# Gated linear attention: each head's norm follows in pieces during the next head's scan, and the output projection's first tile takes its input tiles as they are finished

## The chip, the core and the metric

The kernel runs on one core of a Trainium2 chip. The metric is the device time of one execution in microseconds (us). The four compute engines of the core work in parallel, each on its own list of instructions in order, and wait for one another through semaphores: TensorE (PE, matrix multiplies; its weight loads are listed apart as PEld), VectorE (DVE), ScalarE (ACT) and GpSimd (POOL). SyncE (SP) issues the DMAs that bring the weights. Everything is float32; the profile has two records for each float32 matmul.

## What is computed

The program is a two-layer backbone over 256 context tokens and 256 latent tokens: layer 0 is a bidirectional chunked gated linear attention (GLA) and a dense SwiGLU, layer 1 a bidirectional RWKV-7 mixer and a top-2-of-8 mixture of experts (MoE). The change is in GLA alone. Cut to what matters:

```
def gla_chunk_scan(q, k, v, log_a, s0):            # chunks of 64 tokens
    def step(s, inp):
        b = cumsum(log_a of the chunk);  q_dec = qc * exp(b)
        att = where(mask, q_dec @ (kc * exp(-b)).T, 0)
        y = att @ vc + q_dec @ s
        s = s * exp(b_last) + (kc * exp(b_last - b)).T @ vc
        return s, y

def finish(y, r):                                  # y: sum of both directions, per head 256 values
    yn = y * rsqrt(mean(y * y, axis=-1) + NORM_EPS) * norm_g
    return (yn.reshape(..., 1024) * silu(r)) @ w_out
```

There are 4 heads of 128 keys and 256 values. What `finish` does for a head needs that head's scan alone; the product with `w_out` sums over all heads.

## The kernel before

Activations lie with features on the 128 partitions and the 512 tokens (context, then latent) along the row, so a tensor of 1024 features is 8 tiles of 128x512. The GLA result is `Y1`, tiles 2h and 2h+1 for head h.

**The scan of a head.** TensorE computes the masked-to-be scores of both directions into PSUM banks `ps[0]` and `ps[1]` (L802, 8 matmuls), VectorE masks and adds them (L1765, L1768, L1771), and TensorE multiplies them with the values into `ps[2]` and `ps[3]` (L810). Then follow 8 steps, i = 0 to 7, with both directions in each. In a step TensorE computes the two state updates of the chunk (L821, into `ps[4]` to `ps[7]`), VectorE makes the new state from the old one and the update (L1781 in step 0, L1784 after that), and from step 1 on TensorE adds the part of the output that the state gives (L831). An update of the state waits until TensorE has read the old one, and L831 of the next step waits for the new one. When step 7 is through, ScalarE copies the two banks to `Y1` (L1378).

**The norm.** It begins when all four heads are scanned and copied. For each head in turn: ScalarE squares the two tiles into `sq` (L1385); TensorE sums the squares over the features with a matrix of ones, two matmuls into `ps[h % 2]` (L840); ScalarE takes the root into the one buffer `std` (L1389); VectorE takes the reciprocal (helper `get_rstd`, L1634) and multiplies twice for each tile: with the reciprocal (L1792), then with the gain and silu(r) (L1793, which counts `fn_done` up). ScalarE's root for a head waits for `fn_done` of the head before it, since `std` is one buffer.

**The projection.** The helper `project` (matmuls at L735) makes 8 output tiles of 8 matmuls each. Before its first one stands a wait for all 8 `fn_done`. From the third tile on it has a sum of squares for the next norm between tiles (helper `stat`, L660). ScalarE empties each tile (helper `empty`, L1333). Weights come through a ring of six slots of 1 MB; SP issues a chunk at L479 when TensorE has finished with the chunk six places before it. The MoE weights have rings of their own, filled from L495 and L502 in the same way.

The order of work is the order in which the code stands, engine by engine; there is no scheduler.

## Time and profile before

| what | value |
|---|---|
| median of 3 runs | 2488.49 us (2486.59 to 2490.86) |
| the profiled execution, its own time | 2480.1 us |
| its span, first to last instruction | 2478.3 us |
| TensorE busy | 2267.4 us, 91% of the span |
| VectorE busy | 657.1 us, 27% |
| ScalarE busy | 454.4 us, 18% |
| mean granted TensorE clock | 0.959 of full |

The profile is one execution. Shares are averages over stages with different limits. From about 1515 us on the MoE weights stream in at up to 407 GB/s; the GLA scan and norm lie between 268 and 375 us, in which hardly a byte is moved. A matmul's busy time is modelled at its end, so neighbouring matmul rows overlap a little; the distance between their starts is the better measure of the pace. Line numbers (L802) are those of the kernel before unless said otherwise.

### The profile page before, as it was taken

Reading aid. Unit: us, or ns where it says so; the run is one execution under the profiler, and the core shown is the slowest. Engines: PE = TensorE matmul, PEld = TensorE weight load, DVE = VectorE, ACT = ScalarE, POOL = GpSimd, SP = SyncE. Lnnn points to the kernel's source line nnn. Section 1 sums busy time; section 2 is a strip of 40 time slices with the busy share of each in tenths; the row PEclk is TensorE's granted clock in tenths of the full one; section 3 lists DMA queues with packets and bytes.
Section 4 is the critical chain, followed back from the end, with each engine's and each line's share of the span. In section 5 each row is a group of like instructions: output and inputs, shape, how many; then the busy total and the mean of one; then the engine's idle time right before and its main releaser. Section 6 shows DMA issues by size and latency. Waiting matters only on the chain.

```text
span 2478.3 us, 43079 instructions
## 1 busy us (share of the span) xinstructions
PE 2267.4 (91%) x19363; PEld 1416.9 (57%) x19364; DVE 657.1 (27%) x1175; ACT 454.4 (18%) x771; POOL 48.5 (2%) x165
## 2 busy tenths in 40 slices
PE   6999879899999999897997997989999989999986
PEld 3474644344446877787877876433776333875332
DVE  1032450400000034776467753210000101000102
ACT  3134111200000116453424433000000000000001
POOL 0000000400000000000000000000000000000000
PEclk8999889999999999999999998999999989999998
DMA  7254101522223362102340025899998999999994
GB/s 260 85 184 164 60 1 51 191 98 68 85 68 119 138 233 94 46 4 74 126 153 4 5 80 222 330 407 407 406 359 302 407 407 407 398 321 339 407 407 196
DMA packets 181951, 502.60 MB, mean 203 GB/s; under 512 B 9571, under 2 KB 73381, under 8 KB 175621
## 3 DMA queue, kind: packets, MB, share of 16 engines
q1 hardware_dynamic: 180148, 494.27, 53.5%
q0 software_dynamic: 1616, 5.54, 0.7%
q8 instruction: 155, 2.54, 0.4%
q14 instruction: 32, 0.25, 0.0%
HBM read 498.72 MB, written 1.05 MB: 202 GB/s over the span
## 4 chain that ended last, share of the span: by engine, by line
PE 40%; DMA 6%; SPq 6%; DVE 4%; issue 2%; ACT 1%; DVEq 0%; ACTq 0%
PE banks L968 8%; PE banks L1224 7%; PE banks L1243 7%; PE banks L1186 7%; DMA ring_arena<-in_moe_w_gu 6%; SPq L495 4%; PE banks L735 3%; SPq L502 2%; PE banks L1197 1%; PE banks L1209 1%; PE banks L1120 1%; PE banks L1179 1%; PE banks L915 1%; DVE ring_arena L1987 1%; PE banks L928 1%
## 5 line engine op out<-in xcount | busy, mean ns | idle before, releaser
L1186 PE MATMUL banks<-ring_arena 128*64 128x448 f32 x1536 | 320.2, 567 | 46.6 <-DMA ring_arena<-in_moe_w_gu 46.6
L735 PE MATMUL banks<-ring_arena 128*128 128x256 f32 (+1 forms) x1024 | 314.9, 466 | 15.4 <-DVE ring_arena L1793 9.3
L872 PE MATMUL banks<-ring_arena 128*128 128x512 f32 x704 | 305.4, 597 | 6.4 <-ACT ring_arena L1308 6.1
L735 PEld LDWEIGHTS banks<-ring_arena 128*128 128x128 f32 x1024 | 195.5, 192 | 134.2 <-issue 102.0
L1224 PE MATMUL banks<-ring_arena 128*64 128x512 f32 (+1 forms) x896 | 251.5, 605 | 7.0 <-DVE ring_arena L2204 7.0
L1186 PEld LDWEIGHTS banks<-ring_arena 128*64 128x64 f32 x1536 | 110.4, 142 | 237.3 <-issue 220.6
L968 PE MATMUL banks<-ring_arena 64*64 64x128 f32 (+1 forms) x6144 | 203.6, 256 | 35.9 <-DVE ring_arena L1992 19.1
L872 PEld LDWEIGHTS banks<-ring_arena 128*128 128x128 f32 x704 | 134.7, 192 | 176.3 <-issue 175.2
L968 PEld LDWEIGHTS banks<-ring_arena 64*64 64x64 f32 x6144 | 191.1, 135 | 42.7 <-issue 29.2
L1224 PEld LDWEIGHTS banks<-ring_arena 128*64 128x64 f32 (+1 forms) x896 | 90.5, 149 | 153.0 <-issue 151.9
L1243 PEld LDWEIGHTS banks<-ring_arena 128*64 128x64 f32 x3584 | 171.8, 137 | 9.4 <-issue 9.2
L1243 PE MATMUL banks<-ring_arena 128*64 128x112 f32 x3584 | 174.8, 259 | 0.0
L885 PE MATMUL banks<-ring_arena 128*128 128x256 f32 x704 | 157.5, 380 | 0.8 <-DVE ring_arena L1808 0.8
L885 PEld LDWEIGHTS banks<-ring_arena 128*128 128x128 f32 x704 | 133.0, 190 | 26.1 <-issue 6.7
L2212 DVE TENSOR_TENSOR ring_arena<-ring_arena,banks 128x448 f32<-128x448 f32 x24 | 14.9, 621 | 457.9 <-PE banks L1186 457.9
L1333 ACT ACTIVATE ring_arena<-banks 128x256 f32<-128x256 f32 (+2 forms) x94 | 40.1, 440 | 293.6 <-PE banks L735 178.5
L1494 ACT COPY ring_arena<-banks 128x1024 f32<-128x1024 f32 (+1 forms) x80 | 72.3, 928 | 111.2 <-DVE ring_arena L1987 98.2
L1595 ACT ACTIVATE ring_arena<-banks 128x448 f32<-128x448 f32 x24 | 13.0, 544 | 392.2 <-PE banks L1186 392.2
L1808 DVE TENSOR_TENSOR ring_arena<-ring_arena,banks 128x512 f32<-128x512 f32 x22 | 15.0, 686 | 260.3 <-PE banks L872 260.3
L2217 DVE TENSOR_TENSOR ring_arena<-ring_arena,banks 128x448 f32<-128x448 f32 (+1 forms) x16 | 8.3, 560 | 261.9 <-PE banks L1243 261.9
L1634 DVE RECIPROCAL rstd<-std 128x512 f32<-128x512 f32 (+1 forms) x11 | 30.5, 2771 | 145.3 <-ACT std L1292 136.2
L1403 ACT ACTIVATE ring_arena<-banks 128x512 f32<-128x512 f32 x22 | 13.1, 597 | 272.2 <-PE banks L872 272.2
(340 smaller groups left out, 2006.8 us busy)
## 6 DMA issues: line engine op xcount, KB each, us to landing
ring_arena<-in_moe_w_gu SPq DMA_DIRECT2D x256, 896.0 KB, 16.3
ring_arena<-in_moe_w_d SPq DMA_DIRECT2D x112, 1024.0 KB, 17.1
ring_arena<-in_mod_w SPq DMA_DIRECT2D x48, 1024.0 KB, 6.7
ring_arena<-in_ff_w_gu SPq DMA_DIRECT2D x22, 1024.0 KB, 5.1
ring_arena<-in_ff_w_d SPq DMA_DIRECT2D x22, 1024.0 KB, 4.9
ring_arena<-in_rw_w_rkv SPq DMA_DIRECT2D x20, 1024.0 KB, 5.3
ring_arena<-in_gla_w_in SPq DMA_DIRECT2D x12, 1024.0 KB, 5.4
ring_arena<-in_gla_w_out SPq DMA_DIRECT2D x4, 1024.0 KB, 6.4
```

Source lines behind the costliest of these rows:

```text
L495: sp.dma_start(gu_slots[u % GU_RING].rearrange("p (k n) -> p k n", k=2), src).then_inc(gu_in[u % GU_RING], 16)
L502: sp.dma_start(wd_slots[u % WD_RING].rearrange("p (k n) -> p k n", k=2), src).then_inc(wd_in[u % WD_RING], 16)
L735: ins = T.matmul(b[:, 0:width], w[:, k, j * P:j * P + P], src[:, k, :], start=(k == 0), stop=(k == KT - 1))
L872: ins = T.matmul(ps[4 * (p % 2) + 2 * ab + j][:, :], w[:, k, j * P:j * P + P], H2[:, k, :], start=(k == 0), stop=(k == KT - 1))
L885: ins = T.matmul(ps[4 * half + j // 2][:, cols], w[:, k, j * P:j * P + P], HID[:, 2 * i + k, tok_cols(half)], start=(i == 0 and k == 0 and ...
L968: ins = T.matmul(bank[rows[1 - r if cross and p >= HP // 2 else r], p, 0:x.shape[-1]], lhs[rows[r], p, :], x, start=first and p % (HP // 2 ...
L1186: ins = T.matmul(ps[2 * half][slots_at(h, CH), 0:BLOCK], XG[:, 2 * kp + kk, 0:CH], w[:, kk, BLOCK * h:BLOCK * h + BLOCK], start=(kp == 0 a ...
L1224: ins = T.matmul(ps[6 + h][slots_at(h, cap), :], HX[:, 2 * u + k, 0:cap], w[:, k, 512 * h:512 * h + 512], start=(u == 0 and k == 0), stop= ...
L1243: ins = T.matmul(bank[CH * h:CH * h + CH, (c % 4) * CAP:(c % 4) * CAP + cap], w[:, kk, c * P + CH * h:c * P + CH * h + CH], XG[:, 2 * kp + ...
L1333: C.activation(dst, src, func, **kw).then_inc(S["pj_out"], 1)
L1494: C.copy(w[d]["ZT"][:, :, half], scan_banks(d, 0)[:, :, half]).then_inc(za_s[d], 1)
L1634: link(Vv.reciprocal(rstd[:, 0:width], std[:, 0:width]))
```

## The change

Each head's norm moves into the scan of the next head. ScalarE squares a head's tiles directly after it has copied them. TensorE does the head's two sums after the state updates of step 1 of the next head; the last head's are done after its scan, into bank `ps[6]`. VectorE takes the reciprocal of heads 0 to 2 in four pieces of 128 columns, one after the state updates of each of the steps 2 to 5 of the next head, and does the four multiplications after step 6, ahead of the masks of the head after it. The last head's norm has the form it had. TensorE has one new wait, that the root two heads back has read its bank before the scores overwrite it. The projection no longer waits for all eight tiles: `project` has the argument `first_k`, with which the first output tile waits, matmul by matmul, for `fn_done` of the tile that it is about to read.

```
--- before.py
+++ after.py
@@ -294,6 +294,9 @@
         def turned_at(c, h):
 
             return ps[1 + 2 * h][:, CH * (c % 4):CH * (c % 4) + CH]
+
+        def head_sum_bank(h):
+            return ps[h % 2] if h < GH - 1 else ps[6]
 
         def slots_at(h, cap):
 
@@ -794,9 +797,18 @@
             pe.wait_ge(S["kd_t_out"], 8)
 
 
+            def head_sums(h):
+
+                for vt in range(2):
+                    pe.wait_ge(S["fn_sq"], 2 * h + vt + 1)
+                    T.matmul(head_sum_bank(h)[:, :], ones[:, :], sq[:, vt * TOK:vt * TOK + TOK],
+                             start=(vt == 0), stop=(vt == 1)).then_inc(S["fn_ss"], 1)
+
             for h in range(GH):
                 if h >= 1:
                     pe.wait_ge(S["att_out"], 2 * h)
+                if h >= 2:
+                    pe.wait_ge(S["fn_std"], h - 1)
                 for d in range(2):
                     for t in range(4):
                         ins = T.matmul(ps[d][:, t * P:t * P + P], KI[d][:, h, t * P:t * P + P],
@@ -822,6 +834,8 @@
                                      KDT[d][r0:r0 + CH, c // 2, h * P:h * P + P],
                                      V[r0:r0 + CH, c // 2, h * GDV:h * GDV + GDV],
                                      start=True, stop=True).then_inc(S["sup"], 1)
+                    if i == 1 and h >= 1:
+                        head_sums(h - 1)
                     if i >= 1:
                         for d in range(2):
                             n = (NCH - 1) * h + i
@@ -834,13 +848,10 @@
                             ins.then_inc(S["sinter"], 1)
 
 
-            for h in range(GH):
-                for vt in range(2):
-                    pe.wait_ge(S["fn_sq"], 2 * h + vt + 1)
-                    T.matmul(ps[h % 2][:, :], ones[:, :], sq[:, vt * TOK:vt * TOK + TOK],
-                             start=(vt == 0), stop=(vt == 1)).then_inc(S["fn_ss"], 1)
-            pe.wait_ge(S["fn_done"], KT)
-            project(first["gla_o"], Y1, TOK, 4, lambda n: stat(1, n - 2, TOK) if n >= 2 else None)
+            head_sums(GH - 1)
+            pe.wait_ge(S["fn_std"], GH - 1)
+            project(first["gla_o"], Y1, TOK, 4, lambda n: stat(1, n - 2, TOK) if n >= 2 else None,
+                    lambda k: pe.wait_ge(S["fn_done"], k + 1))
             stat(1, 6, TOK)
             stat(1, 7, TOK)
 
@@ -1376,17 +1387,13 @@
                 act.wait_ge(S["sinter"], 2 * (NCH - 1) * (h + 1))
                 for vt in range(2):
                     C.copy(Y1[:, 2 * h + vt, :], ps[2 + vt][:, :]).then_inc(S["y_out"], 1)
-
-            act.wait_ge(S["y_out"], 2 * GH)
-            for h in range(GH):
+                act.wait_ge(S["y_out"], 2 * h + 2)
                 for vt in range(2):
-                    if h >= 1:
-                        act.wait_ge(S["fn_ss"], 2 * h)
                     C.activation(sq[:, vt * TOK:vt * TOK + TOK], Y1[:, 2 * h + vt, :], ACT.Square).then_inc(S["fn_sq"], 1)
                 act.wait_ge(S["fn_ss"], 2 * h + 2)
                 if h >= 1:
                     act.wait_ge(S["fn_done"], 2 * h)
-                C.activation(std[:, :], ps[h % 2][:, :], ACT.Sqrt, scale=1.0 / GDV, bias=EPS).then_inc(S["fn_std"], 1)
+                C.activation(std[:, :], head_sum_bank(h)[:, :], ACT.Sqrt, scale=1.0 / GDV, bias=EPS).then_inc(S["fn_std"], 1)
             for k in range(KT):
                 empty(O1[:, k, :])
                 act.wait_ge(S["pj_out"], tile[0])
@@ -1757,6 +1764,21 @@
                     dve.wait_ge(S["kd_t"], n + 1)
                     Vv.tensor_copy(KDT[d][:, t, :], ps[6 + n % 2][:, :]).then_inc(S["kd_t_out"], 1)
 
+            def head_rstd(h, part):
+
+                dve.wait_ge(S["fn_std"], h + 1)
+                cols = slice(P * part, P * part + P)
+                link(Vv.reciprocal(rstd[:, cols], std[:, cols]))
+
+            def head_scaled(h):
+
+                for vt in range(2):
+                    k = 2 * h + vt
+                    g = VEC["gla_norm_g"] + vt
+                    link(Vv.tensor_tensor(Y1[:, k, :], Y1[:, k, :], rstd[:, :], ALU.mult))
+                    Vv.scalar_tensor_tensor(Y1[:, k, :], Y1[:, k, :], vecs[:, g:g + 1], R[:, k, :],
+                                            ALU.mult, ALU.mult).then_inc(S["fn_done"], 1)
+
             for h in range(GH):
                 dve.wait_ge(S["att"], 2 * h + 1)
                 if h >= 2:
@@ -1784,14 +1806,12 @@
                             ins = Vv.scalar_tensor_tensor(ST[:, d, :], ST[:, d, :], DEC[d][:, h, c:c + 1], upd,
                                                           ALU.mult, ALU.add)
                         ins.then_inc(S["snew"], 1)
-            for h in range(GH):
-                get_rstd(h, TOK, "fn_std")
-                for vt in range(2):
-                    k = 2 * h + vt
-                    g = VEC["gla_norm_g"] + vt
-                    link(Vv.tensor_tensor(Y1[:, k, :], Y1[:, k, :], rstd[:, :], ALU.mult))
-                    Vv.scalar_tensor_tensor(Y1[:, k, :], Y1[:, k, :], vecs[:, g:g + 1], R[:, k, :],
-                                            ALU.mult, ALU.mult).then_inc(S["fn_done"], 1)
+                    if h >= 1 and 2 <= i < 6:
+                        head_rstd(h - 1, i - 2)
+                if h >= 1:
+                    head_scaled(h - 1)
+            get_rstd(GH - 1, TOK, "fn_std")
+            head_scaled(GH - 1)
             dve.wait_ge(S["csil"], 2)
             Vv.tensor_copy(csil[1][:, :, :], csil[0][:, :, :]).then_inc(S["csil"], 1)
             post(1, O1, TOK, 0, 0, (0, 1))
```

On TensorE, this is the start of the second head before: masked scores times values (L810), then the steps' updates (L821) and outputs (L831).

```order
L802 MATMUL banks<-ring_arena 128x128 x8
L810 MATMUL banks<-ring_arena 128x128 x8
L821 MATMUL banks<-ring_arena 128x256 x4
L831 MATMUL banks<-ring_arena 128x64 x4
L821 MATMUL banks<-ring_arena 128x256 x2
```

And the same place now (L814, L822, L833 and L845 are the same lines further down, L804 the sums):

```order
L814 MATMUL banks<-ring_arena 128x128 x8
L822 MATMUL banks<-ring_arena 128x128 x8
L833 MATMUL banks<-ring_arena 128x256 x4
L804 MATMUL banks<-sq_ntmp,ones 128x512 x2
L845 MATMUL banks<-ring_arena 128x64 x4
L833 MATMUL banks<-ring_arena 128x256 x2
```

Two matmuls of 512 columns now stand between the updates and the outputs of step 1, in heads 1, 2 and 3.

On VectorE, this is the second head before and the masks of the third: masks (L1765 to L1771), first states (L1781), later states (L1784).

```order
L1765 TENSOR_TENSOR ring_arena<-banks,masks 128x512
L1768 TENSOR_TENSOR ring_arena<-banks,masks 128x512
L1771 TENSOR_TENSOR ring_arena<-ring_arena 128x512
L1781 COPY ring_arena<-banks 128x256 x2
L1784 SCALAR_TENSOR_TENSOR ring_arena<-ring_arena,banks 128x256 x12
L1765 TENSOR_TENSOR ring_arena<-banks,masks 128x512
```

And now, from the second head's states on (L1803 and L1806 are the states, L1771 a piece of the reciprocal, L1778 and L1779 the multiplications, L1787 the next head's first mask):

```order
L1803 COPY ring_arena<-banks 128x256 x2
L1806 SCALAR_TENSOR_TENSOR ring_arena<-ring_arena,banks 128x256 x4
L1771 RECIPROCAL rstd<-std 128x128
L1806 SCALAR_TENSOR_TENSOR ring_arena<-ring_arena,banks 128x256 x2
L1771 RECIPROCAL rstd<-std 128x128
L1806 SCALAR_TENSOR_TENSOR ring_arena<-ring_arena,banks 128x256 x2
L1771 RECIPROCAL rstd<-std 128x128
L1806 SCALAR_TENSOR_TENSOR ring_arena<-ring_arena,banks 128x256 x2
L1771 RECIPROCAL rstd<-std 128x128
L1806 SCALAR_TENSOR_TENSOR ring_arena<-ring_arena,banks 128x256 x2
L1778 TENSOR_TENSOR ring_arena<-ring_arena,rstd 128x512
L1779 SCALAR_TENSOR_TENSOR ring_arena<-ring_arena,vecs 128x512
```

After these two come two more multiplications, and only then the masks of the third head.

## Rows read from the trace of the kernel before

**Rows 1.** Page, first part: engine, busy us, share, instructions.
```profile
PE 2267.4 (91%) x19363; PEld 1416.9 (57%) x19364; DVE 657.1 (27%) x1175; ACT 454.4 (18%) x771; POOL 48.5 (2%) x165
```

**Rows 2.** Windows: stretch, length, busy per engine, granted clock, DMA share, GB/s.
```profile
323.54:340.98 17.44, 15.67 (x118) 12.64 (x117) 8.40 (x17) 1.07 (x2) 0.00 (x0) 1.00 0.01 1
340.98:374.49 33.51, 14.41 (x17) 4.29 (x17) 24.65 (x21) 9.00 (x15) 0.00 (x0) 0.66 0.00 0
```

**Rows 3.** Timeline of TensorE: start, length, instruction, [idle before <- releaser].
```profile
273.89 3.39 PE L810 MATMUL banks<-ring_arena 128*128 128x128 f32 x16 [1.51 <-DVE ring_arena L1771]
...
292.50 2.05 PE L810 MATMUL banks<-ring_arena 128*128 128x128 f32 x16 [1.51 <-DVE ring_arena L1771]
294.49 1.13 PE L821 MATMUL banks<-ring_arena 64*128 64x256 f32 x8
295.70 1.10 PE L831 MATMUL banks<-ring_arena 128*128 128x64 f32 x8
...
339.88 1.10 PE L831 MATMUL banks<-ring_arena 128*128 128x64 f32 x8 [0.18 <-DVE ring_arena L1784]
342.80 3.78 PE L840 MATMUL banks<-sq_ntmp,ones 128*128 128x512 f32 x4 [1.82 <-ACT sq_ntmp L1385]
...
374.49 16.29 PE L735 MATMUL banks<-ring_arena 128*128 128x512 f32 x32 [9.26 <-DVE ring_arena L1793]
...
391.47 7.03 PE L735 MATMUL banks<-ring_arena 128*128 128x512 f32 x16
```

**Rows 4.** Timeline of VectorE, same columns.
```profile
287.51 0.93 DVE L1784 SCALAR_TENSOR_TENSOR ring_arena<-ring_arena,banks 128x256 f32<-128x256 f32 x2 [0.74 <-PE banks L831]
290.14 0.69 DVE L1765 TENSOR_TENSOR ring_arena<-banks,masks 128x512 f32<-128x512 f32 x1 [1.70 <-PE banks L802]
291.03 0.69 DVE L1768 TENSOR_TENSOR ring_arena<-banks,masks 128x512 f32<-128x512 f32 x1 [0.20 <-PE banks L802]
...
298.12 0.93 DVE L1784 SCALAR_TENSOR_TENSOR ring_arena<-ring_arena,banks 128x256 f32<-128x256 f32 x2 [0.74 <-PE banks L831]
...
347.25 3.35 DVE L1634 RECIPROCAL rstd<-std 128x512 f32<-128x512 f32 x1 [6.98 <-ACT std L1389]
...
351.36 0.75 DVE L1793 SCALAR_TENSOR_TENSOR ring_arena<-ring_arena,vecs 128x512 f32<-128x512 f32 x1
...
352.75 0.75 DVE L1793 SCALAR_TENSOR_TENSOR ring_arena<-ring_arena,vecs 128x512 f32<-128x512 f32 x1
```

**Rows 5.** Timeline of ScalarE, same columns.
```profile
343.29 1.28 ACT L1389 ACT_TABLE_LOAD   x1
346.62 0.60 ACT L1389 ACTIVATE std<-banks 128x512 f32<-128x512 f32 x1 [2.05 <-PE banks L840]
...
383.95 0.60 ACT L1333 ACTIVATE ring_arena<-banks 128x512 f32<-128x512 f32 x1 [15.80 <-PE banks L735]
```

**Rows 6.** Groups by form: VectorE's reciprocals; count, busy us, mean ns.
```profile
L1634 DVE RECIPROCAL rstd<-std 128x512 f32<-128x512 f32 x7 | 23.5, 3353 | 100.3 <-ACT std L1292 91.1 <-ACT std L1389 9.2
L1634 DVE RECIPROCAL rstd<-std 128x256 f32<-128x256 f32 x4 | 7.0, 1753 | 45.0 <-ACT std L1292 45.0
```

**Rows 7.** Windows, read for the granted clock (third figure from the end).
```profile
290.99:292.50 1.51, 0.00 (x1) 0.00 (x0) 1.38 (x2) 0.00 (x0) 0.00 (x0) 1.00 0.05 11
342.80:346.60 3.80, 3.78 (x4) 1.17 (x4) 0.00 (x0) 1.75 (x2) 0.00 (x0) 0.50 0.00 0
378.40:380.40 2.00, 2.00 (x5) 0.77 (x5) 0.00 (x0) 0.00 (x0) 0.00 (x0) 0.82 0.00 0
443.20:446.00 2.80, 0.02 (x1) 0.02 (x1) 2.69 (x5) 0.63 (x1) 0.00 (x0) 1.00 1.02 415
447.50:450.50 3.00, 3.00 (x10) 0.50 (x2) 2.86 (x7) 0.71 (x2) 0.00 (x0) 0.50 1.07 362
```

**Rows 8.** Waits of SP's DMA queue: total us, times, longest.
```profile
SPq L479 <- PE banks L735: 179.1, 4, 133.8
...
SPq L495 <- PE banks L1123: 50.3, 1, 50.3
```

## The prediction

> **What bounds the kernel now.** I read the page's busy shares first: TensorE is busy 91% of the span [rows 1], so a change pays where it takes away time in which TensorE stands still or runs slowly. Next, the windows from the scan's last head to the projection [rows 2]. In a head of the scan (17.44 us) TensorE is busy 15.67 us at full clock. In the norm (33.51 us) it does 8 matmuls, which show 14.41 us of busy time because they run at the lower clock level for the most part (0.66 granted on average); VectorE has 24.65 of the 33.51. So the norm is a serial walk over four heads: the timelines show it, in a cycle of square, sum, root, reciprocal, four multiplications [rows 3 to 5]. The projection begins at 374.49, released by VectorE's last multiplication.
>
> Then I asked who is late inside the scan, since the work goes there. A step lasts 0.93 + 0.74 = 1.67 us: VectorE works 0.93 and waits 0.74 for TensorE [rows 4]. TensorE sets the pace; the room on VectorE is 0.74 us a step. Last, SP's queue [rows 8]: from 375 to 640 us the weight DMAs wait for TensorE to free a slot, and over the whole trace the first MoE chunk waits 50.3 us for TensorE's L1123. No transfer is waited for at the projection, and the later streams start when TensorE's own progress lets them; a shift here should reach the end of the program.
>
> **The change, part by part.** I count from E, the end of the last scan matmul (339.88 + 1.10 = 340.98), to the end of the projection's first tile, which ScalarE begins to empty at 383.95 [rows 3, 5]. That is E + 42.97.
>
> *The tail now.* Only head 3 is left in it, and its chain up to its reciprocal is head 0's of today: squares, then sums from E + 1.82 to E + 5.60 (342.80 and 3.78), root from E + 5.64 to 6.24, reciprocal to E + 9.62, first tile scaled at E + 11.13 (351.36 + 0.75), second at E + 12.52 (352.75 + 0.75) [rows 3 to 5]. Head 2's multiplications (2.90, below) begin some 0.7 us before E and are done by E + 2.2, before head 3's root, so they hold nothing up. The projection's first six matmuls need only heads 0 to 2 and can start at E + 5.60. At full clock a matmul of 512 columns is 7.03 / 8 = 0.88 us (the row at 391.47 has 16 records, 8 matmuls). A matmul of the projection's start today is slower: the first tile takes 383.9 - 374.49 = 9.4 us instead of 7.0, and the clock is back at full by about 379 (0.82 in 378.4 to 380.4) [rows 3, 7]. In the new tail TensorE works without a break from E + 1.82, so most of the slow stretch falls on the sums; I add 0.5 us for what is left. Six matmuls: 5.3 + 0.5, to E + 11.4. The seventh finds its tile ready (11.13) and ends at 12.3; the eighth waits to 12.57 and ends at 13.45. Saved: 42.97 - 13.45 = 29.5 us. With sums at full clock (1.76 instead of 3.78) it would be 31.5.
>
> *Sums in the scan.* Two matmuls a head, 1.76 us, between updates and outputs of step 1. Today the outputs start 0.08 us after the updates end (294.49 + 1.13 to 295.70) [rows 3], so nothing but that gap hides them: 1.68 us in each of heads 1, 2 and 3, 5.0 us. Bounds: 5.0 at full clock, 3 x 3.7 = 11.1 if each ran at the pace of row 342.80.
>
> *Reciprocal in pieces.* No row has 128 columns. 512 take 3.353 us and 256 take 1.753 [rows 6]: 1.600 for 256 columns, so 0.153 fixed and 0.80 for 128, 0.95 us. It lies between half the 256 row (0.88) and the whole (1.75); I take 0.95, as the two rows make a line. With 0.03 us of linking a step on VectorE is 0.93 + 0.95 + 0.03 = 1.91 against 1.67: 0.24 late a step, four steps, 0.96 us. TensorE has some slack inside a step, but step 7's outputs wait for step 6's state today already (the idle of 0.18 before 339.88 [rows 3]), so the whole 0.96 comes out at the head's end. Three heads: 2.9 us. Bounds: 4 x 0.14 = 0.56 a head (0.88 a piece, 1.7 us in all) and 4 x 1.04 = 4.2 a head (12.5 in all).
>
> *Multiplications before the next masks.* 347.25 + 3.35 = 350.60 to 353.50 is 2.90 us for a head's four [rows 4]. Today VectorE's last states end at 288.44 and the first mask starts at 290.14, after waiting 1.70 for the scores. Now it starts 1.2 us later; the second mask need no longer wait its 0.20, so the masked scores, and with them TensorE's L810, come 1.05 us later. This happens ahead of heads 2 and 3 (after head 3 it lies in the tail): 2.1 us. Bounds: 1.2 and 2 x 2.9 = 5.8, if the scores came as late as the multiplications end.
>
> *ScalarE's work* (copies, squares, root) lies in time that it spends waiting for TensorE, over half of each head. Sqrt loads a table, once in the norm (1.28 us), during TensorE's sums [rows 5]; squares and copies after it show no second load, up to the emptying at 383.95. So I count nothing for mixing the functions. The Trainium skill, ScalarE: Activation LUTs, on table sets, speaks against interleaving: activation calls should be batched by set, since each change of set costs a load, given as about 2.7 us. By that, with copy, square and root taken in turn, each head might pay a load or two; the trace disagrees for this mix, and its one load is 1.28 us. Even at the page's figure it would lie beside TensorE's scores, values and updates, 290.14 to 295.6 in head 1.
>
> *The clock in the scan.* The new wait before L810 makes TensorE's gap there 1.51 + 1.05 = 2.56 us ahead of heads 2 and 3. A gap of 1.51 left the clock at 1.00; after the gap of 2.80 at 443.2 it was 0.50 from 447.5 to 450.5; after the last head and 1.82 of idling, 0.50 [rows 7]. So 2.56 lies nearer the cases that lost it, and I take it as lost in both places. L810 at the low level is 3.39 us against 2.05 [rows 3]: 1.34 each, 2.7 us. Bounds: nothing, and 4.5 us a place if it lasts over the first steps and the sums (1.34 + 2.02 for the sums + about 1.1 for the steps between, an estimate from the same ratio), 9 in all.
>
> *Sum.* 29.5 - 5.0 - 2.9 - 2.1 - 2.7 = 16.8 us. Against the profiled execution: span 2478.3 - 16.8 = 2461.5, its own time (1.8 more) 2463.3. The median of the runs stands 8.4 above that execution; a difference carries over, so the forecast is 2488.5 - 16.8 = 2471.7.
>
> **Rivals.**
>
> *The clock holds.* If neither gap costs the full clock, and the tail's sums run at it, the gain is 29.5 + 2.0 - 10.0 = 21.5, and 19.5 if only the gaps are harmless: 2467.0 to 2469.0. For it: the last head of the scan, its gap included, shows 1.00 [rows 2]. Against: the gaps grow by 70%.
>
> *VectorE becomes the bound.* If pieces and links are dearer (1.3 us a piece instead of 0.95, 0.59 late a step, 7.1 us in three heads), or the low clock reaches the sums in both heads (9 instead of 2.7), the gain is 12.6 or 10.5: 2475.9 to 2478.0. For it: VectorE's 0.74 of room is smaller than any piece. Against: the line through the two reciprocal rows is tight.
>
> *The gain is given back later.* A later stage could be tied to something this shift doesn't move. The time would be within 5 us of 2488.5. Against it stand rows 8, and that hardly a byte moves in the norm; the 407 GB/s stage starts when TensorE frees it.
>
> *The scan falls to the low clock and stays.* The pieces make TensorE idle a little in four steps of each head and much at two head starts. The two places of the scan that ran at both levels give a ratio of 3.39 / 2.05 = 1.65. Three heads of 15.67 us busy at that ratio are 30.6 us more, the three sums 6.1 more; 5.0 of it covers what VectorE adds. Instead of 19.5 won, 12.2 are lost: 2500.7. It decides against the change once the low stretch holds 19.5 / 0.65 = 30 us of full-clock work, some two heads. Against it: head 0 began at the low level (L810 at 3.39), and the scan left it by itself: head 3 is at 1.00 [rows 2, 3]. The Trainium skill, TensorE: Matmul & The Clock Gate, on psum-queue depth-cycling, says that brief idling between groups of matmuls can be frequent enough to make the clock oscillate and to lose throughput by it; the scan today has such idling at every head and shows 1.00 in its gap and over head 3, so the trace does not bear that out here, and it would need the added gaps to matter.
>
> **How the numbers follow.** Forecast (gain 14 to 19) 0.60; the clock holds 0.20; VectorE or a longer low clock 0.13; given back later 0.04; the scan at low clock 0.03. Runs of before differ by 2 us about their median and the profiled one by 8, so I widen by 2 to 3 at either end: 2464 to 2479 leaves out the last two rivals and the outer edges of the others, less than 2 in 10. Faster than before by over 0.2% (5 us, about what runs of this kernel can tell from none) 0.93, within it 0.04, slower 0.03.
>
> **What would show it.** In the profile after: from the last scan output to the first projection matmul about 5.6 us instead of 33.5, and to the first emptying 13.4 instead of 43; heads 1 to 3 longer by 2.6, 5.0 and 5.0 us (with the transition and the clock put to the head that follows); reciprocals of 128 columns at 0.95 us; a wait of about 2.5 us before the scores times values in heads 2 and 3, with a granted clock below 1 after it; one table load; stretches after the projection as long as before. I would be wrong if the steps with a piece stay at 1.67 us, if the clock never falls in the scan, or if the MoE stage lasts longer by what was saved.

## The result, and the profile after

The changed kernel takes 2465.7 us (median of 5 runs, 2456.97 to 2469.02), the kernel before 2486.59 us (5 runs): the medians differ by 20.9 us. The ratio on record, which isn't the quotient of the two medians, is 0.9909 with a 95% interval of 0.9887 to 0.9931; on the time of before that is 22.6 us, between 17 and 28. A second set gave 0.9910 (0.9880 to 0.9940), with medians 19.1 us apart. The forecast was 16.8 us, a ratio of 0.9932. It was 4 us too small by the medians and 6 by the ratio. The parts of the change do what was forecast; three terms of the sum, overlap on VectorE twice and the clock once, were wrong, as is worked out behind the experiments.

The profiled execution took 2465.7 us, its span is 2464.0. Against the span of before that is 14.3 us, less than the runs say. Of the 20.3 us that the stage itself gained (below), 1.3 were lost in head 0, before anything is changed (head 1 begins at 290.28 instead of 288.99), and 4.7 after the first emptying; what lies behind is in the first experiment.

TensorE's timeline, with start, length, instruction and [idle before <- releaser], answers to [rows 3] (L814, L822, L833, L845, L738 are L802, L810, L821, L831, L735 of before; L804 are the sums):

```profile
290.28 2.00 PE L814 MATMUL banks<-ring_arena 128*128 128x128 f32 x16
293.80 2.05 PE L822 MATMUL banks<-ring_arena 128*128 128x128 f32 x16 [1.51 <-DVE ring_arena L1793]
295.78 1.14 PE L833 MATMUL banks<-ring_arena 64*128 64x256 f32 x8
296.84 1.98 PE L804 MATMUL banks<-sq_ntmp,ones 128*128 128x512 f32 x4
298.66 1.00 PE L845 MATMUL banks<-ring_arena 128*128 128x64 f32 x8
299.59 0.70 PE L833 MATMUL banks<-ring_arena 64*128 64x256 f32 x4
...
308.65 1.10 PE L845 MATMUL banks<-ring_arena 128*128 128x64 f32 x8 [0.65 <-DVE ring_arena L1806]
309.59 2.00 PE L814 MATMUL banks<-ring_arena 128*128 128x128 f32 x16
313.74 3.46 PE L822 MATMUL banks<-ring_arena 128*128 128x128 f32 x16 [2.15 <-DVE ring_arena L1793]
...
335.28 2.05 PE L822 MATMUL banks<-ring_arena 128*128 128x128 f32 x16 [2.15 <-DVE ring_arena L1793]
...
350.13 1.10 PE L845 MATMUL banks<-ring_arena 128*128 128x64 f32 x8 [0.65 <-DVE ring_arena L1806]
353.06 3.78 PE L804 MATMUL banks<-sq_ntmp,ones 128*128 128x512 f32 x4 [1.83 <-ACT sq_ntmp L1392]
356.64 15.18 PE L738 MATMUL banks<-ring_arena 128*128 128x512 f32 x32
```

Two rows of before that belong beside them, the start of head 1 and its updates of step 2:

```profile
288.99 2.00 PE L802 MATMUL banks<-ring_arena 128*128 128x128 f32 x16
...
296.74 0.70 PE L821 MATMUL banks<-ring_arena 64*128 64x256 f32 x4
```

The projection starts 5.4 us after the last scan output (351.23 to 356.64) instead of 33.5. The sums stand almost fully on the path: outputs of step 1 start 2.88 us after the updates instead of 1.21, which is 1.67 more. The outputs are then followed sooner than before, so the updates of step 2 start 3.81 us after those of steps 0 and 1 (295.78 to 299.59) instead of 2.25 (294.49 to 296.74): 1.56 us more. The wait before step 7's outputs has grown from 0.18 to 0.65, the one before the values from 1.51 to 2.15 in heads 2 and 3, and in head 2 the values (L822) take 3.46 us instead of 2.05.

The windows of heads 1, 2, 3 and of the stretch to the projection, columns as in [rows 2]:

```profile
290.28:309.59 19.31, 17.15 (x122) 13.38 (x122) 12.22 (x22) 4.11 (x6) 0.00 (x0) 1.00 0.00 1
309.59:331.13 21.54, 18.74 (x123) 14.86 (x122) 14.15 (x25) 2.82 (x5) 0.00 (x0) 0.92 0.00 1
331.13:351.23 20.10, 17.30 (x122) 13.40 (x121) 14.27 (x26) 2.82 (x5) 0.00 (x0) 1.00 0.00 1
351.23:356.64 5.41, 3.58 (x6) 1.51 (x6) 1.98 (x3) 2.22 (x4) 0.00 (x0) 0.54 0.00 0
```

Of the three heads only head 2 lost clock (0.92). VectorE's timeline answers to [rows 4]:

```profile
300.98 0.93 DVE L1806 SCALAR_TENSOR_TENSOR ring_arena<-ring_arena,banks 128x256 f32<-128x256 f32 x2 [0.74 <-PE banks L845]
301.82 0.94 DVE L1771 RECIPROCAL rstd<-std 128x128 f32<-128x128 f32 x1
302.80 0.87 DVE L1806 SCALAR_TENSOR_TENSOR ring_arena<-ring_arena,banks 128x256 f32<-128x256 f32 x2
303.59 0.95 DVE L1771 RECIPROCAL rstd<-std 128x128 f32<-128x128 f32 x1
304.57 0.87 DVE L1806 SCALAR_TENSOR_TENSOR ring_arena<-ring_arena,banks 128x256 f32<-128x256 f32 x2
...
311.01 0.75 DVE L1779 SCALAR_TENSOR_TENSOR ring_arena<-ring_arena,vecs 128x512 f32<-128x512 f32 x1
311.68 0.68 DVE L1787 TENSOR_TENSOR ring_arena<-banks,masks 128x512 f32<-128x512 f32 x1
312.28 0.68 DVE L1790 TENSOR_TENSOR ring_arena<-banks,masks 128x512 f32<-128x512 f32 x1
...
363.01 0.75 DVE L1779 SCALAR_TENSOR_TENSOR ring_arena<-ring_arena,vecs 128x512 f32<-128x512 f32 x1
```

A step with a piece lasts 302.80 - 300.98 = 1.82 us the first time and 304.57 - 302.80 = 1.77 after that, not 1.91. VectorE shows no wait between its rows there. The helper `link` makes VectorE wait for the result of the instruction just issued; instructions that aren't linked so start up to 0.09 us before the row of the one ahead ends (300.98 + 0.93 = 301.91 against 301.82), and a pair of states takes 0.87 instead of 0.93 (the masks are 0.60 apart). On ScalarE the root's table is loaded once in this stage, in head 1, beside TensorE's work, and the first tile is emptied at 364.98:

```profile
292.76 1.28 ACT L1396 ACT_TABLE_LOAD   x1
...
364.98 0.60 ACT L1344 ACTIVATE ring_arena<-banks 128x512 f32<-128x512 f32 x1 [7.51 <-PE banks L738]
```

### The profile page after: what moved, and what is told of

It is laid out like the page before. It is cut to its first block, busy times and chain, and to the rows that moved or that the text cites. A ratio compares the mean times of both kernels' runs of the same rounds, so it can differ in the third digit from the quotient of the medians.

```text
span 2464.0 us, 43103 instructions
## 1 busy us (share of the span) xinstructions
PE 2267.2 (92%) x19363; PEld 1420.5 (58%) x19364; DVE 655.7 (27%) x1184; ACT 454.9 (18%) x771; POOL 48.5 (2%) x165
## 3 DMA queue, kind: packets, MB, share of 16 engines
HBM read 498.72 MB, written 1.05 MB: 203 GB/s over the span
## 4 chain that ended last, share of the span: by engine, by line
PE 40%; DMA 6%; SPq 6%; DVE 4%; issue 2%; ACT 1%; DVEq 0%; ACTq 0%
PE banks L1235 7%; PE banks L979 7%; PE banks L1254 7%; PE banks L1197 7%; DMA ring_arena<-in_moe_w_gu 6%; SPq L498 3%; PE banks L738 3%; SPq L505 2%; PE banks L1131 1%; PE banks L1208 1%; PE banks L1220 1%; PE banks L1190 1%; DVE ring_arena L2007 1%; PE banks L926 1%; PE banks L939 1%
## 5 line engine op out<-in xcount | busy, mean ns | idle before, releaser
L1197 PE MATMUL banks<-ring_arena 128*64 128x448 f32 x1536 | 320.3, 567 | 47.0 <-DMA ring_arena<-in_moe_w_gu 46.8
L738 PE MATMUL banks<-ring_arena 128*128 128x256 f32 (+1 forms) x1024 | 313.6, 465 | 6.3 <-ACT ring_arena L1344 4.5
L738 PEld LDWEIGHTS banks<-ring_arena 128*128 128x128 f32 x1024 | 195.1, 192 | 124.0 <-issue 101.1
L979 PEld LDWEIGHTS banks<-ring_arena 64*64 64x64 f32 x6144 | 190.4, 135 | 45.8 <-issue 31.3
L896 PE MATMUL banks<-ring_arena 128*128 128x256 f32 x704 | 157.5, 380 | 0.8 <-DVE ring_arena L1828 0.8
L778 PE MATMUL banks<-ring_arena 128*128 128x256 f32 x256 | 58.0, 389 | 0.0
```

The source lines that it names most:

```text
L738: ins = T.matmul(b[:, 0:width], w[:, k, j * P:j * P + P], src[:, k, :], start=(k == 0), stop=(k == KT - 1))
L778: ins = T.matmul(b[:, 0:256], H[:, k, t * P:t * P + P], w[:, k, :], start=(k == 0), stop=(k == KT - 1))
L896: ins = T.matmul(ps[4 * half + j // 2][:, cols], w[:, k, j * P:j * P + P], HID[:, 2 * i + k, tok_cols(half)], start=(i == 0 and k == 0 and ...
L979: ins = T.matmul(bank[rows[1 - r if cross and p >= HP // 2 else r], p, 0:x.shape[-1]], lhs[rows[r], p, :], x, start=first and p % (HP // 2 ...
L1197: ins = T.matmul(ps[2 * half][slots_at(h, CH), 0:BLOCK], XG[:, 2 * kp + kk, 0:CH], w[:, kk, BLOCK * h:BLOCK * h + BLOCK], start=(kp == 0 a ...
```

## The experiments

The stage that matters is from head 1's first scores to the first emptying of the projection: 383.95 - 288.99 = 94.96 us before, 364.98 - 290.28 = 74.70 after. Head 0 isn't changed, and is left out. All versions stand in one table, in us: the lengths of heads 1 to 3 (each from its scores to the next head's, the third to the end of the last output, E), the time from E to the first emptying, the stage, what the stage gained over 94.96, and the ratio of the whole kernel to before. The stage is read from one profile of each version, the ratio from all its runs; the last two versions and the one with TensorE fed ran on another chip than the other experiments, each beside runs of before on that chip.

| version | heads 1, 2, 3 | E to emptying | stage | gain of the stage | ratio (95%) |
|---|---|---|---|---|---|
| before | 17.28, 17.27, 17.44 | 42.97 | 94.96 | 0 | 1 |
| before, again | 17.28, 17.27, 17.44 | 43.02 | 95.01 | -0.1 | 0.9993 (0.9978 to 1.0009) |
| changed | 19.31, 21.54, 20.10 | 13.75 | 74.70 | 20.3 | 0.9909 (0.9887 to 0.9931) |
| changed, again | 19.30, 20.23, 21.55 | 13.59 | 74.67 | 20.3 | 0.9910 (0.9880 to 0.9940) |
| waits for all tiles | 19.30, 20.20, 21.57 | 21.09 | 82.16 | 12.8 | 0.9954 (0.9939 to 0.9970) |
| tile-by-tile waits alone | 17.27, 17.28, 17.43 | 34.35 | 86.33 | 8.6 | 0.9955 (0.9938 to 0.9972) |
| whole reciprocal | 24.74, 28.18, 26.69 | 13.75 | 93.36 | 1.6 | 1.0002 (0.9991 to 1.0013) |
| the same, TensorE fed | 21.02, 23.31, 23.46 | 12.97 | 80.76 | 14.2 | 0.9941 (0.9927 to 0.9956) |
| masks first | 20.02, 20.23, 19.57 | 13.74 | 73.56 | 21.4 | 0.9917 (0.9900 to 0.9934) |
| sums in the gap | 18.00, 18.94, 18.97 | 13.75 | 69.66 | 25.3 | 0.9900 (0.9883 to 0.9916) |
| both moves | 17.99, 18.00, 18.71 | 13.75 | 68.45 | 26.5 | 0.9897 (0.9880 to 0.9914) |
| and pieces spread | 17.83, 17.83, 17.99 | 13.03 | 66.68 | 28.3 | 0.9869 (0.9854 to 0.9884) |
| and squares first | 17.57, 17.57, 17.74 | 10.81 | 63.69 | 31.3 | 0.9883 (0.9868 to 0.9898) |

**Both kernels again, unchanged.**

> The kernel before, unchanged, for a second profile and a second set of times. In the first pair of profiles the change is 20.3 us at the end of the projection's first tile once the same start is taken for the scan (19.0 as read, 1.3 of it lost in head 0 before anything is changed), but the spans differ by 14.3 alone. Theory A (chance placement of TensorE's low clock in later stages): this execution shows the same GLA rows to 0.1 us, apart from where the clock rises in head 0, and its later stages differ from the first profile of the same kernel by some 2 to 6 us, with low-clock stretches in other places. Theory B (the change gives back some 5 us later): the later stages repeat to within 1 us, and the kernel with the change always loses there. Time: no difference from before.

> The kernel with the change, unchanged. Theory A: from the projection's first emptying to the end of the span it takes what the kernel before takes, within the few us that the clock's places make; 20 to 22 us faster than before by the medians. Theory B: 14 to 16 us faster. In the scan I expect heads of 19.3 us (head 1) and 20.0 (heads 2 and 3) at full clock, and 1.4 to 1.6 more where the clock falls in the wait before the values; it may fall in head 3 this time, or in neither.

The ratios are in the table. The profiles, from the first emptying to the end (before, before again, changed; columns as in [rows 2]):

```profile
383.95:2478.30 2094.35, 1940.65 (x18024) 1226.50 (x18022) 543.08 (x1018) 360.61 (x646) 44.45 (x146) 0.97 0.58 218
```

```profile
381.40:2477.80 2096.40, 1947.29 (x18024) 1229.66 (x18022) 542.65 (x1018) 360.78 (x646) 44.57 (x146) 0.96 0.58 217
```

```profile
364.98:2464.00 2099.02, 1944.65 (x18024) 1228.84 (x18022) 542.69 (x1018) 360.71 (x646) 44.40 (x146) 0.96 0.58 217
```

The rest of the program is the same code in every version of the table and takes 2094.4 to 2105.0 us by their thirteen profiles; in the changed kernel's second profile 2096.6. The kernel before differs from itself by 2.1 us there, and TensorE's busy time for the same 18024 records by 6.6; of the 4.7 us that the change's first profile is longer, 4.0 are TensorE's busy time. So theory A holds: one pair of spans tells the gain to no better than some 5 us, while the stage repeats to 0.05 us. Theory B (14 to 16 us by the medians, always lost in the rest) falls. A loss of a us or two later can't be told from this spread. Theory A's 20 to 22 us by the medians was missed by a little: they are 19.1 apart, and the ratio says 22. In this second profile of the change the clock is lost elsewhere, at the ends of heads 2 and 3. The wait of 2.15 before head 2's values is there as before, and the values after it take 2.05:

```profile
311.88 2.05 PE L822 MATMUL banks<-ring_arena 128*128 128x128 f32 x16 [2.15 <-DVE ring_arena L1793]
...
326.73 1.43 PE L845 MATMUL banks<-ring_arena 128*128 128x64 f32 x8 [0.65 <-DVE ring_arena L1806]
327.95 3.35 PE L814 MATMUL banks<-ring_arena 128*128 128x128 f32 x16
```

**The last part undone, and alone.**

```
-            pe.wait_ge(S["fn_std"], GH - 1)
-            project(..., lambda k: pe.wait_ge(S["fn_done"], k + 1))
+            pe.wait_ge(S["fn_std"], GH - 1)
+            pe.wait_ge(S["fn_done"], KT)
+            project(...)                        # all tiles; the reverse edit in the kernel before
```

> The change without its last part: the projection waits for all eight tiles. Theory (the waits tile by tile let six matmuls run beside the last head's root, reciprocal and multiplications): the projection starts 12.5 us after the last scan output instead of 5.4, with the clock down, as before the change (9.4 us for the first tile), so the first tile ends at 21.9 instead of 13.75: 8 us slower than the full change, 12 to 13 us faster than before. Rival (the first tile is short anyway and the next tiles catch up, so the part is worth nothing): as fast as the full change, 20 to 22 us faster than before.

> The kernel before with only the last part: norms stay behind the scan, the first output tile waits tile by tile. Theory: last sums end at 365.2, six matmuls to about 372.8, the last two tiles come at 373.0 and 374.4, first tile done at 375.3 instead of 383.9: 8 to 9 us faster than before, so the two parts of the change overlap hardly at all (8 + 12). Rival (the waits are worth nothing while VectorE is the serial part, since the last reciprocal decides): the first tile ends within 1.5 us of before.

Undone, the projection starts at E + 12.49 as expected, and the first emptying is at E + 21.09, where 21.9 was expected: 7.3 to 7.5 us later than with the part. Alone it makes the stage 8.6 us shorter:

```profile
362.92 5.96 PE L735 MATMUL banks<-ring_arena 128*128 128x512 f32 x12
370.71 1.12 PE L735 MATMUL banks<-ring_arena 128*128 128x512 f32 x2 [1.83 <-DVE ring_arena L1794]
372.10 7.99 PE L735 MATMUL banks<-ring_arena 128*128 128x512 f32 x18 [0.26 <-DVE ring_arena L1794]
```

The first six matmuls (12 records) run beside the last head's reciprocal; then the seventh waits 1.83 us and the eighth 0.26. Moving the norms alone gains 12.8 us of the stage, the waits alone 8.6: 21.4 as a sum, 20.3 measured together, so the two parts overlap by 1.1 us. Both rivals fall.

**The reciprocal whole.**

```
-                    if h >= 1 and 2 <= i < 6:
-                        head_rstd(h - 1, i - 2)
+                    if h >= 1 and i == 2:
+                        get_rstd(h - 1, TOK, "fn_std")
```

> The change with the reciprocal of heads 0 to 2 whole (512 columns, 3.35 us) after step 2 of the next head, instead of four pieces after steps 2 to 5. Theory (the pieces fit mostly into VectorE's 0.74 us of room per step, and show only 0.47 us a head): step 3's state comes 2.6 us late, TensorE absorbs 0.4, so heads 1 to 3 get about 1.7 us longer each, 5 us in all, and TensorE has a gap of 2 us in the step, which can cost the clock another 1 to 2 us a head. Rival (three more fixed costs of 0.15 us a head are what the pieces cost, and the room in the later steps swallows the rest): equal or 1 us faster than the change.

By the runs the whole gain is gone (ratio 1.0002; the stage keeps 1.6 us of it), where 5 us were expected to go, or up to 11 with the clock. TensorE in head 1:

```profile
299.56 0.70 PE L833 MATMUL banks<-ring_arena 64*128 64x256 f32 x4
302.37 1.64 PE L845 MATMUL banks<-ring_arena 128*128 128x64 f32 x8 [2.11 <-DVE ring_arena L1806]
303.95 1.23 PE L833 MATMUL banks<-ring_arena 64*128 64x256 f32 x4
305.10 1.97 PE L845 MATMUL banks<-ring_arena 128*128 128x64 f32 x8
...
311.66 3.73 PE L814 MATMUL banks<-ring_arena 128*128 128x128 f32 x16
```

The wait of 2.11 us is the size that I expected. But the outputs after it take 1.64 and 1.97 instead of 1.10, the updates 1.23 instead of 0.70, and this goes on through the next head's scores (3.73 instead of 2.00). The granted clock of the three heads:

```profile
286.92:311.66 24.74, 21.12 (x122) 16.68 (x122) 12.63 (x20) 4.11 (x6) 0.00 (x0) 0.82 0.00 1
311.66:339.84 28.18, 24.56 (x121) 20.02 (x122) 14.41 (x23) 2.83 (x5) 0.00 (x0) 0.68 0.00 1
339.84:366.53 26.69, 23.08 (x121) 18.34 (x121) 14.61 (x23) 2.82 (x5) 0.00 (x0) 0.76 0.00 1
```

This is the rival of the low clock that stays, in another kernel than the one forecast: three heads are 79.6 us long instead of 61. The Trainium skill (TensorE: Matmul & The Clock Gate, on psum-queue depth-cycling) says that brief idling of TensorE between groups of matmuls, where it is frequent enough, loses throughput through the clock; for this version the trace agrees, with 0.68 to 0.82 granted.

**The same, with TensorE fed in the wait.**

```
+                    if i == 4 and h >= 1:
+                        for vt in range(2):
+                            T.matmul(ps[h % 2][:, :], ones[:, :], sq[:, vt * TOK:vt * TOK + TOK], ...)
```

> As the version with the whole reciprocal, with two more matmuls of 512 columns on TensorE in step 4 of heads 1 to 3, just where it waits 2.11 us for VectorE; their result is not used. That version was 21 us slower than the change where 5 were expected, and its heads (24.7, 28.2 and 26.7 us) show matmuls at the low pace from the wait on. Theory (the low clock after TensorE's wait made the larger part of it, the wait itself 1.6 us a head): with TensorE fed the clock stays at full, heads of 21 to 22 us, from head 1's start to the first emptying 78 us instead of 93.4, and the kernel is 12 to 16 us faster in spite of 5 us more work on TensorE. Rival (the reciprocal's lateness itself is passed on and grows): the heads stay above 24 us.

```profile
300.06 1.99 PE L841 MATMUL banks<-sq_ntmp,ones 128*128 128x512 f32 x4
302.24 1.11 PE L849 MATMUL banks<-ring_arena 128*128 128x64 f32 x8 [0.19 <-DVE ring_arena L1810]
```

With 1.8 us of needless matmuls in each head the stage is 12.6 us shorter (80.76 against 93.36; 78 was expected), the ratios (0.9941 against 1.0002) say 15 us, and the outputs after the place are back at 1.11. So of the 18.7 us that the whole reciprocal cost the stage at least two thirds came through the clock, which still wasn't full in heads 2 and 3. The lateness itself is what head 1 shows with full clock, 21.02 against 19.31: 1.7 us a head, and the rival falls. Head 1 has 21.02 as expected; heads 2 and 3, 23.3 and 23.5, are 1.3 to 1.5 above my range of 21 to 22, with 0.93 granted: their wait before the values is 2.20, and the values after it take 3.05 and 2.52 us.

**Masks ahead of the multiplications.** VectorE does `head_scaled(h - 2)` after the masks of head h, instead of after the states of head h - 1.

> The change with VectorE's order turned at the start of heads 2 and 3: first the new head's masks, then the four multiplications of the head before last. Theory (the multiplications held up the masks by 0.64 us in each of two heads, and the longer wait of 2.15 us is what let the clock fall in head 2): the wait before the values is 1.51 us again in all heads, heads 1 to 3 take 19.3 to 19.5 us each, first states at most 0.15 us late, no low clock in the scan; 1.1 to 2.7 us faster than the change. Rival (the clock falls by its own course whatever the gap): 1.1 us faster at most, and head 2 or 3 still shows L822 at 3.4 us.

The wait before the values is 1.51 us in all heads, and the stage 1.1 us shorter: the first half of the theory holds. The second falls. The clock was lost all the same (0.97 granted over the three heads), at the end of head 1 and in head 2's scores, so the long wait isn't needed for a fall. The rival has the 1.1 us right, and the place wrong: no values took 3.4 us.

```profile
304.45 1.85 PE L845 MATMUL banks<-ring_arena 128*128 128x64 f32 x8 [0.65 <-DVE ring_arena L1808]
306.10 2.93 PE L814 MATMUL banks<-ring_arena 128*128 128x128 f32 x16
```

**Sums between scores and values, and both moves.** The main lines of the edit; the sums in step 1 and the scores' wait for the root go with it.

```
-            return ps[h % 2] if h < GH - 1 else ps[6]
+            return ps[4 + 2 * (h % 2)] if h < GH - 1 else ps[6]
...
                 # after the scores of head h, before the wait for its masks
+                if h >= 1:
+                    pe.wait_ge(S["snew"], 2 * (NCH - 1) * h)
+                    head_sums(h - 1)
...
+                    if h >= 1 and i == 1:
+                        pe.wait_ge(S["fn_std"], h)
```

> The change with each head's two sums moved from step 1 to between scores and values of the next head, where TensorE waits for VectorE's masks; into a bank of the updates. Theory (1.67 us of sums fit into the wait of 1.51 to 2.15 us): the sums end about 0.2 us after the masks in head 1 and before them in heads 2 and 3; heads 1, 2, 3 are 1.4, 1.7 and 1.7 us shorter than in the change, the gap is filled and the clock stays at full; 4.5 to 6.5 us faster than the change. Rival (squares come too late, so the sums wait in the gap and then delay the values by as much): no gain or a loss of 1 us.

> Both of these: sums between scores and values, and masks ahead of the multiplications; ScalarE's root no longer waits for the multiplications, which the order on VectorE makes needless. Theory: gains add up, heads 1 to 3 about 18.0 us each (17.3 before, plus 0.2 of sums and 0.47 of pieces), last scan output about 6.5 us earlier than in the change; about 28 us faster than before. Rival (the root then comes while VectorE multiplies, both are late for step 0's states): heads of 19 us, no better than the sums moved alone.

```profile
283.16 2.00 PE L812 MATMUL banks<-ring_arena 128*128 128x128 f32 x16
285.24 1.96 PE L804 MATMUL banks<-sq_ntmp,ones 128*128 128x512 f32 x4
287.04 1.95 PE L823 MATMUL banks<-ring_arena 128*128 128x128 f32 x16
```

Values of head 1 now start 3.88 us after the scores, against 3.52 without sums: 1.8 us of sums cost 0.36. Head 1 is 1.3 us shorter (18.00); heads 2 and 3 are at 18.94 and 18.97, and over the three heads some clock is lost again (0.97). The stage gained 5.0 us over the change, inside the 4.5 to 6.5, and the rival falls. The whole kernel shows it only weakly: the ratios 0.9900 and 0.9910 are 2.5 us apart and their intervals overlap. With both moves heads 1 and 2 are 18.0 as forecast (the rival had 19), head 3 is 18.71 with 0.97 granted, and the stage gains 6.2 over the change, about the sum of the two (5.0 + 1.1). By the runs 2456.6 and 2457.3 us can't be told apart.

**Pieces spread, then squares first.**

```
-                    if h >= 1 and 2 <= i < 6:
-                        head_rstd(h - 1, i - 2)
+                    if h >= 1 and i in (0, 1, 3, 5):
+                        head_rstd(h - 1, (0, 1, 3, 5).index(i))
```

> As the version with both moves, but the four pieces of the reciprocal stand after the states of steps 0, 1, 3 and 5 instead of 2 to 5. Theory (a piece that has a free step behind it is absorbed: 0.10 late in one step, TensorE has about 0.38 of slack inside it): the wait of 0.65 us before step 7's outputs goes back to 0.18, heads 1 to 3 are 0.47 us shorter each, 17.5 us at full clock, 1.4 us faster than both moves. Rival (VectorE is late for the first states, since the multiplications end just before them, and a piece at step 0 pushes that on): heads 2 and 3 as long as without spreading.

> As the spread version, and ScalarE squares a head's tiles straight from PSUM before it copies them. Theory: the last sums start 0.7 us after the last scan output instead of 1.8, so TensorE's wait there is 1.1 us shorter, and the whole tail with it (first emptying at 12.6 instead of 13.75); if the clock holds over the shorter wait the sums take 1.8 us instead of 3.8 and the first emptying comes at 10.6. 1 to 3 us faster than the spread version, about 27 us faster than before. Rival (the tail is bound by VectorE's chain from the root on, the second pair's wait eats it): less than 0.5 us.

Spreading took the wait before step 7's outputs from 0.65 to 0.34, not 0.18, since step 6's state still follows directly on a piece; heads 1 and 2 are 17.83, 0.16 shorter rather than 0.47. The theory is half right, and its rival (heads 2 and 3 no shorter) falls. The tail is 0.7 us shorter too (13.03), since the last sums take 3.06 us instead of 3.78; nothing in the edit aims at that. Squaring straight from PSUM gave more than a shorter wait:

```profile
338.40 1.10 PE L846 MATMUL banks<-ring_arena 128*128 128x64 f32 x8 [0.34 <-DVE ring_arena L1806]
340.19 1.98 PE L804 MATMUL banks<-sq_ntmp,ones 128*128 128x512 f32 x4 [0.69 <-ACT sq_ntmp L1390]
342.01 5.31 PE L738 MATMUL banks<-ring_arena 128*128 128x512 f32 x12
347.76 1.13 PE L738 MATMUL banks<-ring_arena 128*128 128x512 f32 x2 [0.44 <-DVE ring_arena L1777]
```

The wait after the scan is 0.69 instead of 1.83, the clock is granted in full (1.00 from E on), the last sums take 1.98 us instead of the 3.0 to 3.8 of every other version with the norms moved, and the first emptying comes 10.81 us after E; 10.6 was expected, if the clock holds. In the heads the values start 3.56 us after the scores, with the sums between them at next to no cost, so the heads are 17.57, 0.3 above the kernel before, with the norms of heads 0 to 2 inside. By stage this is the best, 31.3 us. By the runs (4 each) the spread version has 2452.0 us and this one 2454.8, with overlapping intervals; the 3 us between their stages don't show against the spread of the rest, so the 1 to 3 us that I expected between them aren't shown for the whole kernel. By the ratios both beat before by 29 to 33 us and the change by 7 to 10.

## What of the prediction held, and which steps failed

The forecast named what bounds the stage and where each part of the change would cost or gain, and the rows bear that out. Its gain was too small because three terms failed: the pieces of the reciprocal, the multiplications before the masks, and the clock in the scan.

*What bounds, and the tail.* Right. 29.5 us were to be saved from E to the first emptying, 29.2 were. Every event of the last head's chain is within 0.1 us of the forecast but the end, at 13.75 instead of 13.45. The eighth matmul needs VectorE's last multiplication, which ended at 363.01 + 0.75 = 363.76, E + 12.53 (12.52 forecast). From there to the emptying it is 1.22 us, where I had counted 0.93. The low clock at the tile's start (0.72 granted from 356.64 to 360.00) costs nothing here: TensorE had done seven matmuls by the time VectorE was through.

*Sums in the scan.* 1.68 us a head forecast. The outputs come 1.67 later, but the next updates 1.56 (3.81 - 2.25), which is what reaches the head's end: 4.7 us in all, not 5.0.

*Reciprocal in pieces.* The piece was right, 0.946 us against 0.95. The step that failed is the overlap: I added 0.93, 0.95 and 0.03 as if no row overlapped another, and got 0.24 late a step. Measured is 0.15 in the first of the four steps (1.82 - 1.67) and 0.10 in the others (1.77 - 1.67), which fits the growth of the wait before step 7's outputs, 0.65 - 0.18 = 0.47 a head. That is 1.4 in all, not 2.9. With the sums it makes up head 1: 1.56 + 0.47 = 2.03 = 19.31 - 17.28.

*Multiplications before the masks.* The same step failed: 1.05 forecast, 0.64 measured (2.15 - 1.51), as VectorE went from the last states through the four multiplications to the masks without a wait, its unlinked rows overlapping. That is 1.3 us, not 2.1.

*The clock in the scan.* This step failed in its cause as well as its size. The wait that was to be 2.56 us became 2.15. 2.7 us were forecast for two falls in the waits before heads 2 and 3; 1.6 measured in one profile and 1.7 in the other (60.95 and 61.08 us for the three heads, against 19.31 + 19.94 + 20.10 = 59.35 with no loss; 19.94 is head 3's length less the 0.16 by which a next head's scores start before the last output ends). There was one fall in the first, in head 2's wait as I had it, none in head 3's equal wait, and two in the second, at other places. The mechanism that I gave, a gap long enough, doesn't decide it: after 2.15 us the clock fell in one case of four (heads 2 and 3 of the first profile, head 2 of the second and of the version that waits for all tiles), and with the wait back at 1.51 it was lost anyway. That the two sizes lie within 1.1 us is luck. What does decide is open. Of the versions in the table, the scan has 1.00 granted in all five with 0.18 or 0.34 us before step 7's outputs and no longer wait elsewhere (both profiles of before, the waits alone, spread, squares first), and some loss in all six with 0.65; that is a pattern over single profiles, no test, since no version changed that wait alone.

*Sum.* 29.2 - 4.7 - 1.4 - 1.3 - 1.6 = 20.2, with 20.3 read from the stage. Three terms were too dear, by 3.4 us together: pieces (1.5) and multiplications (0.8) because I added lengths without their overlap, the clock (1.1) because I counted a fall in each of two waits. The sums in the scan (0.3 too dear) and the tail (0.3 too good) cancel. The ratio's 22.6 us has an interval of 17 to 28, which holds the stage's 20.3.

*ScalarE.* One table load, nothing on the path. *Given back later:* no; TensorE waits for the MoE weights as long as before (46.8 us in all against 46.6), and the rest of the program costs the same within its spread. *The clock holds:* half, for a head or two at a time. *VectorE becomes the bound:* it did in four steps of a head, but by 0.10 to 0.15 us each. *The low clock stays:* not in this kernel; in its neighbour with one longer wait it came back in every head. The prediction's ratio of 1.65 for the low level was too small, since the row of 3.39 us ran in part at full clock: in that neighbour the outputs show 1.97 / 1.10 = 1.8 and the scores 3.73 / 2.00 = 1.9.

## What to carry to other kernels

When work is moved onto an engine that has some room in each step, cut it so that a piece is about the room: four pieces of 0.95 us in a room of 0.74 cost 0.47 us a head here, one of 3.34 cost over 6 us a head more, two thirds of it through TensorE's clock. A free step between pieces gave 0.16 us a head back. Back-to-back instructions on VectorE overlapped a little (up to 0.09 us), so price a filled step by the start-to-start distance of rows that stand close, not by the sum of their lengths. Check a cost at the end of the loop step and not only at the next row: the sums looked like 1.67 us and were 1.56. And put extra matmuls where TensorE waits already: the same sums cost 1.56 us in the loop and 0.36 or less in the wait beside it.

## What was not expected of the hardware

Two needless matmuls of 512 columns per head made a stage 12.6 us shorter, by keeping TensorE's granted clock up (0.95 instead of 0.75 over three heads) in a wait of 2.11 us; the runs of the two versions, 15 us apart, agree. And profiles of identical code from the first emptying to the end differ by over 10 us (2094.4 to 2105.0), more than most single edits here are worth; a stage's own rows are what tells them apart.
